# Norm tile by tile among the matrix products, and adaLN modulation one tile per chunk over eight phases with 16 tiles in the prelude

## The reference

```python
c_act = jax.nn.silu(c)
for layer in range(2):                              # first_block
    mod = (c_act @ ada_w[layer] + ada_b[layer]).reshape(B, 3, 3, D_MODEL)
    shift, scale, gate = mod[:, :, 0], mod[:, :, 1], mod[:, :, 2]
    h = rms_norm(x, norm_g[layer, 0]) * (1.0 + scale[:, 0]) + shift[:, 0]
    x = x + 0.5 * gate[:, 0] * swiglu(h, ffn_w_in[layer, 0], ffn_w_down[layer, 0])
    h = rms_norm(x, norm_g[layer, 1]) * (1.0 + scale[:, 1]) + shift[:, 1]
    y = diff_attention(h, ...) if layer == 0 else hgrn2(h, ...)
    x = x + gate[:, 1] * y
    h = rms_norm(x, norm_g[layer, 2]) * (1.0 + scale[:, 2]) + shift[:, 2]
    x = x + 0.5 * gate[:, 2] * swiglu(h, ffn_w_in[layer, 1], ffn_w_down[layer, 1])
for i in range(2):                                  # second_block
    h = rmsnorm(x, norm_mix[i])
    x = x + (sliding_window_attention(h, ...) if i == 0 else short_gated_conv(h, ...))
    x = x + peer_ffn(rmsnorm(x, norm_ffn[i]), ...)
```

## Time and profile before

| | |
|---|---|
| median of the three runs | 3588.69 us (3579.77 to 3588.9) |
| the profiled execution | 3586.82 us, span of its trace 3584.4 us |
| mean granted clock of TensorE | 0.921 |
| PE busy | 3003.4 us, 84% of the span |
| DVE busy | 2309.0 us, 64% |
| ACT busy | 1371.9 us, 38% |
| GpSimd busy | 498.3 us, 14% |
| read from HBM | 604.04 MB, 178 GB/s over the span |

### The profile page before, as it was taken

One profiled execution on the slowest core, in us unless ns is written; L12 is line 12 of the kernel. 1 busy time (PEld: TensorE's weight loads), 2 busy tenths in 40 slices (PEclk: granted clock), 3 DMA queues, 4 the chain that ended last, 5 costly groups with the idle time before them and its releaser, 6 DMA issues.

```text
span 3584.4 us, 48021 instructions
## 1 busy us (share of the span) xinstructions
PE 3003.4 (84%) x18518; PEld 2646.4 (74%) x18518; DVE 2309.0 (64%) x3078; ACT 1371.9 (38%) x1347; POOL 498.3 (14%) x244
## 2 busy tenths in 40 slices
PE   1987537978986569855799999999877999999998
PEld 1776326867775558644699999888666999998887
DVE  5985555867645746445489787556554797874565
ACT  1433223434435134322344443444333444344443
POOL 0420001302200002000078100000000582000000
PEclk9999758989998789876899999999988999999999
DMA  6985204776543025420345566567543455665675
GB/s 232 344 277 177 78 0 147 268 241 229 205 158 117 0 98 185 152 71 1 132 166 184 200 217 216 189 240 283 203 141 111 166 181 189 224 221 188 238 275 201
DMA packets 146097, 640.20 MB, mean 179 GB/s; under 512 B 12057, under 2 KB 45889, under 8 KB 89409
## 3 DMA queue, kind: packets, MB, share of 16 engines
q1 hardware_dynamic: 127584, 572.12, 46.2%
q10 hardware_dynamic: 18400, 66.59, 5.1%
HBM read 604.04 MB, written 34.62 MB: 178 GB/s over the span
## 4 chain that ended last, share of the span: by engine, by line
PE 75%; DVE 14%; ACT 4%; DMA 4%; issue 3%; POOL 0%; DVEq 0%; SPq 0%; ACTq 0%
PE pp L436 19%; PE pp L438 10%; PE pp L547 7%; PE pp L548 7%; PE pp L549 7%; PE mz L614 6%; PE mz L616 6%; PE mz L617 6%; PE mz L590 2%; DVE ada_raw L1017 2%; PE mz L428 2%; DVE gsq L1078 2%; DMA ada_raw<-ada 1%; DVE w_lo L988 1%; ACT w_hi L737 1%
## 5 line engine op out<-in xcount | busy, mean ns | idle before, releaser
L988 DVE TENSOR_TENSOR w_lo<-raw,w_hi 128x2048 fp32r<-128x2048 f32 (+1 forms) x422 | 923.9, 2190 | 482.3 <-ACT w_hi L737 481.4
L737 ACT ACTIVATE w_hi<-raw 128x2048 fp32r<-128x2048 f32 (+1 forms) x486 | 894.5, 1841 | 511.2 <-DMA raw<-expert_v 366.1
L436 PE MATMUL pp<-hs,w_hi 128*128 128x512 f32 x2400 | 863.0, 404 | 123.2 <-DVE hs L1037 116.7
L438 PE MATMUL pp<-hs,w_lo 128*128 128x256 f32 x2400 | 678.5, 283 | 0.0
L436 PEld LDWEIGHTS pp<-hs,w_hi 128*128 128x128 f32 x2400 | 459.1, 191 | 243.6 <-DVE hs L1037 120.7
L547 PE MATMUL pp<-hs,w_hi 128*128 128x256 f32 x2048 | 584.8, 286 | 0.0
L548 PE MATMUL pp<-hs,w_hi 128*128 128x256 f32 x2048 | 579.3, 283 | 0.0
L549 PE MATMUL pp<-hs,w_lo 128*128 128x256 f32 x2048 | 579.1, 283 | 0.0
L1506 POOL TENSOR_TENSOR w_lo<-raw,w_hi 128x2048 fp32r<-128x2048 f32 x64 | 319.2, 4999 | 1224.3 <-ACT w_hi L737 1224.3
L438 PEld LDWEIGHTS pp<-hs,w_lo 128*128 128x128 f32 x2400 | 461.1, 192 | 0.0
L436 PE MATMUL pp<-us,w_hi 128*128 128x512 f32 x960 | 351.8, 409 | 107.2 <-DVE us L1089 74.5
(11 more groups left out here) (245 smaller groups left out, 3219.9 us busy)
## 6 DMA issues: line engine op xcount, KB each, us to landing
raw<-expert_u SPq DMA_DIRECT2D x128, 1024.0 KB, 4.9
raw<-expert_v SPq DMA_DIRECT2D x128, 1024.0 KB, 4.9
raw<-ffn_in SPq DMA_DIRECT2D x88, 1024.0 KB, 4.9
raw<-ffn_down SPq DMA_DIRECT2D x64, 704.0 KB, 4.1
ada_raw<-ada ACTq DMA_DIRECT2D x76, 512.0 KB, 5.4
ada_raw<-ada ACTq DMA_DIRECT2D x22, 1024.0 KB, 6.3
raw<-out_w SPq DMA_DIRECT2D x16, 1024.0 KB, 4.9
raw<-hgrn SPq DMA_DIRECT2D x16, 1024.0 KB, 4.9
```

Of the source, the lines that this page charges most:

```text
L436: mm(outp, w_hi[:, slot, a:a + P], rhs[:, k0 + k].rearrange("p a t -> p (a t)"), start=(k0 + k == 0), stop=False, skip_group_check=True)
L438: last = mm(outp[:, 0:T], w_lo[:, slot, a:a + P], rhs[:, k0 + k, 0, :], start=False, stop=(k0 + k == last_k), skip_group_check=True)
L737: f(w_hi[:, slot, 0:n], raw[:, slot, 0:n], ACT.Copy).then_inc(hi_ready, 1)
L988: v.tensor_tensor(w_lo[:, slot, 0:n], raw[:, slot, 0:n], w_hi[:, slot, 0:n].bitcast(F32), ALU.subtract)\
```

## The change

The chunks, slots and the split of weights stay. What is new:

- **Norm.** ACT squares one or two tiles of x as soon as they are done (`squares`), and PE sums them among the products of the phase that makes them (`sums`). After the reciprocal, DVE and ACT work tile by tile: h of tile k is one instruction (x times gain times 1/rms), ACT makes the high part with the shift as bias, DVE the low part; PE's first tile product of the next phase waits for each tile (`hs_ready` counts tiles). ACT calls a root of one number ahead of the last squares.
- **Gate and x.** In `ffn_down` and out, ACT's copy of the cross half and DVE's addition are gone; DVE adds both PSUM halves to x one after the other (`add_to_x`), with a semaphore between them, and after the split of the next chunk. PE waits for x instead of `evac_done`.
- **Start of `ffn_down`.** PE waits for the first 11 tiles of u, and then for each.
- **Modulation.** 8 steps of 2 tiles in the prelude (16 tiles: shift and scale of norm 0); then 1 tile per chunk in seven phases and 2 per chunk in out 0. The DMA buffer `ada_raw` and `sq` lie elsewhere.
- **PEER's end and the output.** `y_tok` is copied in halves by ACT and DVE, x is added and stored in four pieces.

```diff
-MOD_STEPS = 12
-MOD_PER = {("ffn_in", 0): 2, ("ffn_down", 0): 1, ("ffn_in", 1): 1, ("ffn_down", 1): 1, ("ffn_in", 2): 1}
+MOD_STEPS = 8
+MOD_PER = {("ffn_in", 0): 1, ("ffn_down", 0): 1, ("attn", 0): 1, ("out", 0): 2, ("ffn_in", 1): 1, ("ffn_down", 1): 1,
+           ("ffn_down", 2): 1, ("hgrn", 0): 1}
...
@@ PE @@
-            def norm(n):
-                pe.wait_ge(norm_sq, n + 1)
-                for k in range(KD):
-                    last = mm(mz[:, 0, 0:T], ones, sq[:, k, :], start=(k == 0), stop=(k == KD - 1))
-                last.then_inc(norm_sum, 1)
-                pe.wait_ge(hs_ready, n + 1)
+            def sums(n, a, b):
+                for k in range(a, b):
+                    pe.wait_ge(norm_sq, KD * n + k + 1)
+                    last = mm(mz[:, 0, 0:T], ones, sq[:, k, :], start=(k == 0), stop=(k == KD - 1), skip_group_check=True)
+                if b == KD:
+                    last.then_inc(norm_sum, 1)
...
                 ph = plan[("ffn_down", q)]
-                pe.wait_ge(u_lo, KF * (q + 1))
                 pe.wait_ge(evac_done, ph.evac0)
-                for rp, pair, half, lap in pairs_of(pe, ph):
-                    pe.wait_ge(evac_done, ph.evac0 + rp - 1)
+
+                def tile_of_u(k):
+                    if k == 0 or k >= KF // 2:
+                        pe.wait_ge(u_lo, KF * q + max(k + 1, KF // 2))
+
+                for rp, pair, half, lap in itertools.chain(pairs_of(pe, ph.part(0, 2)), pairs_of(pe, ph.part(2, KD - 2))):
+                    if not isinstance(rp, int) or rp > 1:
+                        pe.wait_ge(x_done, KD * n + rp - 1)
                     for j in range(2):
                         pe.wait_ge(lo_ready, 2 * pair + j + 1)
+                        first = isinstance(rp, int) and rp == 0
+                        if isinstance(rp, int) and rp == KD - 1:
+                            sums(n + 1, *((0, 6), (6, 7))[j])
...
+                sums(n + 1, KD - 1, KD)
...
@@ ACT @@
-            def norm(n):
-                act.wait_ge(x_done, n) if n else act.wait_ge(x_in, 16)
-                f(sq[:], xT[:], ACT.Square).then_inc(norm_sq, 1)
+            def squares(n, a, w):
+                act.wait_ge(x_done, KD * (n - 1) + a + w) if n else act.wait_ge(x_in, 16)
+                f(sq[:, bass.ds(a, w)], xT[:, bass.ds(a, w)], ACT.Square).then_inc(norm_sq, w)
+
+            def norm(n, a):
+                f(small[:, 63:64], eps, ACT.Sqrt)
+                for k in range(a, KD, 2):
+                    squares(n, k, min(2, KD - k))
                 act.wait_ge(norm_sum, n + 1)
                 f(inv_rms[:], mz[:, 0, 0:T], ACT.Sqrt, bias=eps, scale=1.0 / D).then_inc(norm_rms, 1)
-                act.wait_ge(norm_h, n + 1)
-                f(hs[:, :, 0, :], h32[:], ACT.Copy).then_inc(norm_hi, 1)
-                if n in (0, 2, 3):
-                    act.wait_ge(hs_ready, n + 1)
+                for k in range(KD):
+                    act.wait_ge(norm_h, KD * n + k + 1)
+                    f(hs[:, k, 0, :], h32[:, k], ACT.Identity, bias=a_add[:, n, k:k + 1]).then_inc(norm_hi, 1)
...
             def peer(l, n):
-                act.wait_ge(x_done, n)
+                act.wait_ge(x_done, KD * n)
                 act.dma_start(key_t[:], keys[l]).then_inc(keys_in, 16)
-                norm(n)
+                norm(n, KD - 2)
...
@@ DVE @@
                 link(v.reciprocal(inv_rms[:], inv_rms[:]))
-                link(v.tensor_tensor(h32[:], xT[:], inv_rms[:].unsqueeze(1).to_broadcast([P, KD, T]), ALU.mult))
-                for k in range(KD):
-                    last = v.tensor_scalar(h32[:, k], h32[:, k], a_mul[:, n, k:k + 1], a_add[:, n, k:k + 1], ALU.mult, ALU.add)
-                last.then_inc(norm_h, 1)
-                dve.wait_ge(norm_hi, n + 1)
-                v.tensor_tensor(hs[:, :, 1, :], h32[:], hs[:, :, 0, :].bitcast(F32), ALU.subtract).then_inc(hs_ready, 1)
+                for k in range(KD + 1):
+                    if k < KD:
+                        v.scalar_tensor_tensor(h32[:, k], xT[:, k], a_mul[:, n, k:k + 1], inv_rms[:], ALU.mult, ALU.mult).then_inc(norm_h, 1)
+                    if k:
+                        dve.wait_ge(norm_hi, KD * n + k)
+                        v.scalar_tensor_tensor(hs[:, k - 1, 1, :], h32[:, k - 1], a_add[:, n, k - 1:k],
+                                               hs[:, k - 1, 0, :].bitcast(F32), ALU.add, ALU.subtract).then_inc(hs_ready, 1)
+
+            def add_to_x(ps, g, xk, done):
+                v.scalar_tensor_tensor(xk, ps[0], g, xk, ALU.mult, ALU.add).then_inc(x_half, 1)
+                dve.wait_ge(x_half, done + 1)
+                v.scalar_tensor_tensor(xk, ps[1], g, xk, ALU.mult, ALU.add).then_inc(x_done, 1)
```

More of the change, by code:

```diff
@@ L17 @@
+import itertools
 import math
@@ L528, in attention, with out_product @@
                 weigh(HEADS - 1)
-            def out_product(i):
+            def out_product(i, n):
                 pe.wait_ge(mix_lo, i + 1)
-                products(plan[("out", i)], us)
+                ph = plan[("out", i)]
+                for rp, pair, half, lap in each_pair(ph):
+                    for j in range(2):
+                        c = 2 * rp + j
+                        pe.wait_ge(lo_ready, 2 * pair + j + 1)
+                        if c > 1:
+                            pe.wait_ge(x_done, KD * n + 2 * c - 2)
+                        for t in range(2):
+                            last = tile_product(pp[:, j, t], 2 * half + j, t * KD, us, 0, KD, KD - 1)
+                        last.then_inc(w_used, 1)
+                        if c > 1:
+                            sums(n + 1, 2 * c - 4, 2 * c - 2)
+                sums(n + 1, KD - 4, KD)
             def up(ph, q, spread=None, fresh=False):
@@ L631, in _ @@
             pe.wait_ge(evac_done, 1)
-            norm(0)
-            ffn(0)
-            norm(1)
+            sums(0, 0, KD)
+            ffn(0, 0)
             ph = plan[("attn", 0)]
-            products(ph, hs)
+            products(ph, 1)
             pe.wait_ge(evac_done, ph.evac0 + ph.evacs)
@@ L796, in ffn @@
                         load_modulation(ph, 2 * rp + j + 1, 1 - j)
-                    take_cross(ph, ph.evac0 + rp, half, 2 * pair + 2, 1)
+                        if j == 0 and not (isinstance(rp, int) and rp == 0):
+                            squares(n + 1, rp - 1, 1)
             def group_norm(i, src, work, tiles, count):
@@ L933, in _ @@
             split_mix(0, pj[:, 0:KD])
-            products(plan[("out", 0)])
-            norm(2)
-            ffn(1)
-            norm(3)
-            ffn(2)
-            norm(4)
+            out_product(0, 1)
+            norm(2, KD - 2)
+            ffn(1, 2)
+            norm(3, KD - 1)
+            ffn(2, 3)
+            norm(4, KD - 1)
             ph = plan[("hgrn", 0)]
@@ L958, in _ @@
             split_mix(1, pj[:, 0:KD])
-            products(plan[("out", 1)])
-            norm(5)
-            ffn(3)
-            norm(6)
+            out_product(1, 4)
+            norm(5, KD - 2)
+            ffn(3, 5)
+            norm(6, KD - 1)
             ph = plan[("swa", 0)]
@@ L1056, in ffn @@
                         modulation(ph, rp, j)
[L1057 to L1061 removed]
+                    dve.wait_ge(w_used, 2 * pair + 2)
+                    add_to_x([pp[:, half, 0:1, a * T:(a + 1) * T] for a in range(2)], a_gate[:, n, bass.ds(rp, 1)],
+                             xT[:, bass.ds(rp, 1), :], KD * halves_of[n] + rp)
             def out_product(i, n):
@@ L1358, in _ @@
             out_product(0, 1)
+            dve.wait_ge(mods_in, mods_by(plan, "out", 0))
+            tables(2, 3)
             norm(2)
```

170 lines of the change are left out of this document (98 added, 72 removed).

## The result

The changed kernel takes **3399.85 us** (3396.52 to 3407.0) where the kernel before takes 3588.64 in the same rounds: a ratio of 0.948, interval 0.946 to 0.950. The forecast was 3440 with a range of 3412 to 3475, so the direction and most of the places were right, and the gain was 40 us larger than forecast, outside the range. The profiled execution took 3398.3 us with a span of 3396.5, 187.9 less than before.

A forecast was written before the change was run, and what follows sets the result against it. PE bounds the kernel (75% of the chain), so gains lie where it waits or runs slowly: -102 - 5 + 15 - 26 - 15 - 11 - 3 = -147, from 3586.8 to 3440 us; 8 in 10 between 3412 and 3475.

The forecast's parts named there:

- x behind out phases and PEER: Last product to x: norms 5, 7 and 9 gain 8.7 us, PEER's end before norm 8 about 2.
- the start of `ffn_down`: From `ffn_in`'s last chunk to the first pair's end: 9.1 us instead of 18.8 and 18.0, -34 over four.
- Ahead of the squares: From the last product to x, before the norms: gains and losses per norm sum to -5 us.
- The sums: Sums among the products of `ffn_down` and out phases cost PE 3.2 and 0.9 us each, +15 in all.
- The gap: Last squares to the next phase's first chunk's end, ten norms: 169 us against 271, -102.
- last step and eight more, 4.5 us: End of the gap: first output tile's last step plus eight of the second, bounds 3.2 and 5.8 us.
- 8 us given back: In `ffn_down`, late weights and modulation rows take back 8 us of the early start's 34, bounds 0 and 30.
- The clock that stays low: Rival at the norms: clock returns late, each of ten loses about 3 us, +30, 3470; chance 0.14.
- the lock-step: Rival at the norms: DVE and ACT alternate without overlap, 1.5 us per tile, +46, 3486; chance 0.07.
- the slower kernel: Rival in `ffn_down`: PE's wait loop runs at DMA pace; pairs of 12.3 us decide, 13 give 3610; chance 0.02.
- the `ffn_down` bound: Rival in `ffn_down`: weights and DVE bind, the 26 us gain shrinks to about 8, 3458; chance 0.13.
- The clock that never falls: Rival at the norms: PE's idle gap is too short for a fall, nine gain 2.4 us, 3418; chance 0.14.

The follow-up runs named there:

- the second profile: The changed kernel run once more with nothing changed (label `again`): 3402.13 us.
- the other two profiles: Two further executions of the changed kernel, nothing changed against it: 3402.13 us for the second, 3401.76 us for the changed kernel in later rounds.

## Why the forecast was right in kind and 40 us short

**Right.** The prelude (-15, measured -14.5), `ffn_in` 0 (-11; -13.0, of which 2.2 is the fast pace), the sums' spacing (0.23 said, 0.22 measured), x behind out phases and PEER at norms 5, 7, 8 and 9 (10.7 said, 11.3 measured), the output, and the start of `ffn_down`: of the 34 said, 25.8 are waiting that went, and most of the rest the slow first steps, which the kernel that waits for all of u shows again.

**Ahead of the squares: -5 said, -23.0 measured.** This is the step that failed. I took what DVE does at the end of `ffn_down` as a constant behind PE's last product ("the last one stands ahead of x and waits for its DMA until 294.05") and let the two additions lose 0.3. The chain behind x there starts at the landing of a transfer, most often the next phase's second chunk, not at PE's last product. So it covers the sums that now stand among the last products. The waits of norms 1, 3, 4 and 6 sum to 20.4 us before, to 26.1 in the kernel with the sums last (5.6 more, where I had charged 3.9), and to 10.4 and 12.1 in two profiles of the changed kernel: 14 to 16 of the 18 us are this cover. At norms 1 and 3, 6.70 became 2.88 and 9.13 became 3.38.

Norm 6, which has no modulation, fell from 2.29 to 1.08 by it too, and not by shorter instructions. DVE at norm 6, before (PE's last product ended at 1507.27, ACT's copy at 1507.68) and changed (1382.30):

```profile
1506.38 2.29 DVE L988 TENSOR_TENSOR w_lo<-raw,w_hi 128x2048 fp32r<-128x2048 f32 x1 [1.62 <-ACT w_hi L737]
1508.59 0.41 DVE L1002 TENSOR_TENSOR both<-pp,cross 128x256 f32<-128x256 f32 x1
...
1378.81 2.29 DVE L1039 TENSOR_TENSOR w_lo<-raw,w_hi 128x2048 fp32r<-128x2048 f32 x1 [1.93 <-ACT w_hi L768]
1382.34 0.48 DVE L1094 SCALAR_TENSOR_TENSOR xT<-pp,a_gate,xT 128x256 f32<-128x256 f32 x1 [1.24 <-PE pp L445]
```

Before, the last split held the addition back; now it is done 1.24 us early. The other part of the miss, 3.6 us, is norm 2: I charged 2 and it reads -1.6. The modulation of out 0 costs 1.8 there (3.85 in the second profile, 2.05 in the kernel with the old plan), but I left out the 3.5 that norm 5 gains because the split no longer stands between product and x.

**The sums: +15 said, 4 to 5 in fact.** The same mistake from its other side: I priced the records where they stand and not what waits beside them. Norm 6 pays 1.5, and the out phases 0.5 to 0.9 each; in the kernel with squares and sums in one piece these are 4.8 shorter, of which 1.1 comes back as waiting at norm 2.

**The gap: 15.7 to 22.0 a norm said, 14.2 to 21.2 measured.** The mechanism was right. A tile takes 0.79, not 0.85 (0.4 a norm), and the term "last step and eight more, 4.5 us" was mis-sized: I took it between 3.2 and 5.8 and put the clock's return somewhere in it. It returns before, during the tile by tile steps, and the last part is 0.5 + 2.8 = 3.3. That is 1.2 for each of ten norms; the last sums, two tiles or at half clock, give some 1 to 2 us in all back.

**`ffn_down`: 8 us given back said, 2 to 4 seen.** The pairs stand at 7.6 to 7.8 us; only the last two of `ffn_down` 0 and 2 show 1.7 each beyond the sums, where PE waits for x or its squares (2.0 and 3.8 in all in the other two profiles). The estimated 307 GB/s for the weights and modulation rows was no bound for PE inside the phase; it may show at its end, where a landing holds x.

**The rivals.** The clock that stays low (3470) and the lock-step (3486) are refuted by the rows, the slower kernel (pairs of 12.3 us) too; the `ffn_down` bound (3458) by the pairs. The clock that never falls (3418) came nearest, for the wrong reason: it falls to 0.50, but that costs next to nothing while DVE's 0.79 is longer than a slow step's 0.64. The Trainium skill (TensorE: Matmul & The Clock Gate, "HAM oscillation — how this bites in real kernels") tells of matmul groups that each start slow behind a long wait. The trace agrees for the first piece, which starts at 0.50 behind the idle time; it does not carry over to pieces with short pauses, since the granted clock rose to 1.00 among them. My range ended at 3412 because I moved every uncertain term around a value chosen on the cautious side; the shares of `ffn_down`, sums and x were not independent, since all three hang on the end of `ffn_down`, where landings hold x.

## What to carry to other kernels

Before you charge an instruction on the busiest engine, look what holds the event behind it: work that stands beside a chain which starts elsewhere (here a transfer's landing) is free as far as that chain covers it, and removing it wins nothing. A piecewise hand-over costs what its slowest partner takes per piece; a fallen clock matters only where it makes PE that partner. When several small terms rest on the same transfer, widen the range by their sum, not one by one.

## What the runs showed of the hardware

- At a granted clock of 1.00 a step of 512 and 256 columns takes either 0.3466 or 0.3533 us, constant from one gap to the next and different between executions of one kernel; the 21 later chunks of an `ffn_in` differ by 2.24 us by it. What sets it stayed open.
- From rest the granted clock rose from 0.50 to 1.00 among pieces of work as it does in a closed stream: here between 264 and 265, behind a first step at 260.15. With idle products it stayed at 1.00 at norm 1 across pauses of 1.98 and 0.66 us, and at four other norms; at three it fell all the same (0.50 over 926 to 930).
- A reciprocal of 128x256 on DVE, 1.75 us, is now the longest single link from the last squares to the first step (5.8 us at norm 1).
